# Two edits in the second block: the order of the first weight loads, and how the transposed matrix of the second inverse is made

## The reference

```python
h = rms_norm_2(x, attn_norm_w)
proj = h @ w_in                      # 2048 x 6448: RWKV part (3360 columns), GDN part (the rest)
#   RWKV: r, k, v (3 x 1024), then the low-rank inputs wd, ad, gd (288 columns); GDN: q, k, v, z, a, b
y_a = rwkv7_mixer(p_rwkv, ...)       # a recurrence over the tokens, 16 heads of 64
y_b = gdn_mixer(p_gdn, ...)          # gated delta rule in chunks of 64 tokens, 8 heads of 128:
#   sol = triangular_solve(L + eye, rhs, lower=True, unit_diagonal=True)
x = x + concatenate([y_a, y_b]) @ w_out
x = x + (silu(h2 @ w_gate) * (h2 @ w_up)) @ w_down
```

## Time and profile before

| what | value |
|---|---|
| median of three runs | 2945.02 us (2941.74 to 2945.82) |
| the profiled execution | 2943.11 us, span 2941.4 us |
| TensorE busy | 2876.3 us, 98% |
| VectorE, ScalarE busy | 54%, 40% |
| granted TensorE clock, mean | 0.99 of full speed |
| DMA | 501.12 MB, mean 170 GB/s |

### The profile page before, as it was taken

The page is one execution under the profiler, slowest core; times in us unless marked ns, Lnnn a source line. Parts: engine busy times, 40 slices in busy tenths (PEclk is TensorE's granted clock), DMA queues, the critical chain, the costliest instruction groups (busy, mean ns, idle before and its releaser), DMA issues.

```text
span 2941.4 us, 41822 instructions
## 1 busy us (share of the span) xinstructions
PE 2876.3 (98%) x18274; PEld 2480.6 (84%) x18274; DVE 1600.7 (54%) x1325; ACT 1167.7 (40%) x958; POOL 58.6 (2%) x124
## 2 busy tenths in 40 slices
PE   8999999999999999999998999988899999999998
PEld 7999888888888888888888989988788888888887
DVE  5657555444554455444447657875555445544445
ACT  4345444334443333333335343423344343333333
POOL 0000000000000000002002000000000000000000
PEclk9999999999999999999999999999899999999999
DMA  6555555656555555555565445300255555655554
GB/s 216 163 164 180 161 168 189 197 187 195 186 190 186 185 191 191 188 186 192 194 209 171 158 132 170 101 4 32 86 167 191 186 187 189 195 185 186 198 189 171
DMA packets 257411, 501.12 MB, mean 170 GB/s; under 512 B 12256, under 2 KB 17707, under 8 KB 256891
## 3 DMA queue, kind: packets, MB, share of 16 engines
q1 hardware_dynamic: 257275, 499.06, 52.3%
HBM read 496.74 MB, written 2.10 MB: 170 GB/s over the span
## 4 chain that ended last, share of the span: by engine, by line
PE 94%; DVE 4%; ACT 1%; DMA 1%; issue 0%; SPq 0%; DVEq 0%; ACTq 0%
PE psum L696 23%; PE psum L698 23%; PE psum L697 23%; PE psum L681 5%; PE psum L683 5%; PE psum L684 5%; PE psum L1130 2%; DVE weight_lo L1899 1%; PE psum L747 1%; PE psum L1011 0%; PE psum L642 0%; DMA weight_raw<-in_w_in 0%; ACT weight_hi L1427 0%; PE psum L1017 0%; PE psum L1023 0%; PE psum L996 0%
## 5 line engine op out<-in xcount | busy, mean ns | idle before, releaser
L1899 DVE TENSOR_TENSOR weight_lo<-weight_raw,weight_hi 128x2048 fp32r<-128x2048 f32 x460 | 1054.0, 2292 | 1109.3 <-ACT weight_hi L1427 1108.7
L1427 ACT ACTIVATE weight_hi<-weight_raw 128x2048 fp32r<-128x2048 f32 x460 | 881.4, 1916 | 1509.8 <-PE psum L698 1211.7
L696 PE MATMUL psum<-weight_hi,h_both 128*128 128x512 f32 x1856 | 724.9, 391 | 0.0
L698 PE MATMUL psum<-weight_hi,h_both 128*128 128x512 f32 x1856 | 722.5, 389 | 0.0
L697 PE MATMUL psum<-weight_lo,h_both 128*128 128x512 f32 x1856 | 722.1, 389 | 0.0
L681 PE MATMUL psum<-h_both,weight_hi 128*128 128x256 f32 x1408 | 403.9, 287 | 18.4 <-DVE weight_lo L1899 18.3
L698 PEld LDWEIGHTS psum<-weight_hi,h_both 128*128 128x128 f32 x1856 | 348.3, 188 | 72.8
L697 PEld LDWEIGHTS psum<-weight_lo,h_both 128*128 128x128 f32 x1856 | 348.5, 188 | 71.4
L696 PEld LDWEIGHTS psum<-weight_hi,h_both 128*128 128x128 f32 x1856 | 348.4, 188 | 71.3
L683 PE MATMUL psum<-h_both,weight_lo 128*128 128x256 f32 x1408 | 400.6, 285 | 0.0
L684 PE MATMUL psum<-h_both,weight_hi 128*128 128x256 f32 x1408 | 400.4, 284 | 0.0
(11 more groups left out here) (525 smaller groups left out, 2228.5 us busy)
## 6 DMA issues: line engine op xcount, KB each, us to landing
weight_raw<-in_w_in SPq DMA_DIRECT2D x144, 1024.0 KB, 5.3
weight_raw<-in_w_ffn_in SPq DMA_DIRECT2D x88, 1024.0 KB, 5.0
weight_raw<-in_w_ffn_out SPq DMA_DIRECT2D x44, 1024.0 KB, 5.1
weight_raw<-in_ffn_w_gate SPq DMA_DIRECT2D x44, 1024.0 KB, 5.1
weight_raw<-in_ffn_w_up SPq DMA_DIRECT2D x44, 1024.0 KB, 5.2
weight_raw<-in_ffn_w_down SPq DMA_DIRECT2D x44, 1024.0 KB, 5.1
weight_raw<-in_w_out SPq DMA_DIRECT2D x32, 1024.0 KB, 5.1
weight_raw<-in_w_branch_rnn SPq DMA_DIRECT2D x8, 1024.0 KB, 5.1
```

The lines of the kernel that those rows point to most:

```text
L696: mm(acc[:, t, :], xh[:, c], wh[:, k, :], start=(start and k == 0), stop=False, skip_group_check=True)
L698: last = mm(acc[:, t, :], xl[:, c], wh[:, k, :], start=False, stop=(stop and k == CK - 1), skip_group_check=True)
L1427: A(hi[j % g.hi][:], raw[j % g.ring][:], ACT.Copy).then_inc(hi_ready, 1)
L1899: V.tensor_tensor(lo[r][:], raw[r][:], hi[j % g.hi][:].bitcast(F32), ALU.subtract).then_inc(lo_ready, 1)
```

## The change

In SP's program the order after the fourth chunk becomes: fifth and sixth chunk; wait for `n_sq`; half of the low-rank weights (rows of the first 8 of 16 tiles of 128); seventh chunk; the other half; eighth chunk. The two DMAs become four. ACT does the high parts of chunks five to seven in one go, then waits for all of the low-rank weights (64 instead of 32) and for `x_rescaled`, and splits them in two groups of two. DVE's order there is unchanged.

In the second inverse, for k < 4, the product for the transposed matrix and its addition go, and `chunk_turn` makes the transposed matrix from the new X with a DVE transpose. Its start is made in the same way instead of by `gd_begin`; ACT's copy of `gd_nt` is no longer waited for by DVE. Step 4 stays as it was, but for its semaphores.

```diff
-            load(in2, 0, 0, 4)
+            def load_lora(p0, p1):
+                k = slice(4 * p0, 4 * p1)
+                sp.dma_start(w_lora[:, k, 0:288], w_in2[:, k, 3072:N_RWKV]).then_inc(S("lora_w_landed"), 16)
+                sp.dma_start(w_lora[:, k, 288:LC], w_in2[:, k, 6432:6448]).then_inc(S("lora_w_landed"), 16)
+
+            load(in2, 0, 0, 6)
             sp.wait_ge(n_sq, 16)
-            sp.dma_start(w_lora[:, :, 0:288], w_in2[:, :, 3072:N_RWKV]).then_inc(S("lora_w_landed"), 16)
-            sp.dma_start(w_lora[:, :, 288:LC], w_in2[:, :, 6432:6448]).then_inc(S("lora_w_landed"), 16)
-            load(in2, 0, 4)
+            load_lora(0, 2)
+            load(in2, 0, 6, 7)
+            load_lora(2, 4)
+            load(in2, 0, 7)
...
             def chunk_x(k, b):
                 pe.wait_ge(S("gd_z_out"), 2 * k + b + 1)
-                of_chunks(bank(4 + 2 * b), lambda r, u: xt_gc[r, u, :], lambda r, u: z_gc[r, u, :], 8, 8 * b)
-                of_chunks(bank(5 + 2 * b), lambda r, u: z_gc[r, u, :], lambda r, u: xt_gc[r, u, :], 8, 8 * b).then_inc(S("gd_x"), 1)
+                pe.wait_ge(S("gd_xt_out"), 2 * k + b + 1)
+                last = of_chunks(bank(4 + 2 * b), lambda r, u: xt_gc[r, u, :], lambda r, u: z_gc[r, u, :], 8, 8 * b)
+                if k == 4:
+                    last = of_chunks(bank(5 + 2 * b), lambda r, u: z_gc[r, u, :], lambda r, u: xt_gc[r, u, :], 8, 8 * b)
+                last.then_inc(S("gd_x"), 1)
...
-            chunks(in2, 0, 4, 6)
-            act.wait_ge(S("lora_w_landed"), 32)
+            chunks(in2, 0, 4, 7)
+            act.wait_ge(S("lora_w_landed"), 64)
             act.wait_ge(*at_step("x_rescaled"))
-            lora_high(0, 1)
-            chunks(in2, 0, 6, 7)
-            lora_high(1, 3)
+            lora_high(0, 2)
             chunks(in2, 0, 7, 8)
-            lora_high(3, 4)
+            lora_high(2, 4)
...
+            def chunk_turn(k, b):
+                u = slice(8 * b, 8 * b + 8)
+                dve.wait_ge(S("gd_x_out"), 2 * k + 2 + b + 1)
+                V.transpose(xt_gc[:, u, :], x_gc[:, u, :]).then_inc(S("gd_xt_out"), 1)
...
-                if g == 3:
-                    dve.wait_ge(S("gd_nt_out"), 2)
-                    gd_begin(xt_gc, nt_g, low0_t_c, 0)
+                if g >= 2:
+                    chunk_turn(-1, g - 2)
...
-            dve.wait_ge(S("gd_nt_out"), 4)
-            settle(gd_begin(xt_gc, nt_g, low0_t_c, 1))
...
             def chunk_z(k):
                 for b in range(2):
                     u = slice(8 * b, 8 * b + 8)
+                    if b and k:
+                        chunk_turn(k - 1, 1)
                     dve.wait_ge(S("gd_z"), 2 * k + b + 1)
...
                     dve.wait_ge(S("gd_x"), 2 * k + b + 1)
-                    for o, x in enumerate((x_gc, xt_gc)):
-                        last = V.tensor_tensor(x[:, u, :], x[:, u, :], bank(4 + 2 * b + o).rearrange("p (u n) -> p u n", u=8), ALU.add)
-                    last.then_inc(S("gd_x_out"), 1)
+                    for o, x in enumerate((x_gc, xt_gc) if k == 4 else (x_gc,)):
+                        V.tensor_tensor(x[:, u, :], x[:, u, :], bank(4 + 2 * b + o).rearrange("p (u n) -> p u n", u=8),
+                                        ALU.add).then_inc(S("gd_xt_out" if o else "gd_x_out"), 1)
+                if k < 4:
+                    chunk_turn(k, 0)
```

More of the change, by code:

```diff
@@ L1338, in _ @@
                 pe.wait_ge(S("gd_z_low_out"), b + 1)
+                pe.wait_ge(S("gd_xt_out"), 10 + b + 1)
                 for u in range(8):
@@ L2678, in _ @@
             chunk_x(4)
-            dve.wait_ge(S("gd_x_out"), 12)
+            dve.wait_ge(S("gd_xt_out"), 12)
             V.memset(head_rstd[UP, 0:1], 0.0).then_inc(S("gd_xt_made"), 1)
```

## The result

The changed kernel takes 2922.93 us (median of four runs, 2919.36 to 2929.0), the kernel before 2945.14 us in the same comparison: the ratio is 0.9929, with a 95% interval of 0.9908 to 0.995. That is faster by more than the 0.2% that can be told from no change. The forecast was 2924.2 us. The profiled execution took 2919.36 us, with a span of 2917.7 us; the page answers to the earlier trace rows with

A forecast was written before the change was run, and what follows sets the result against it. TensorE, busy 98% of the span, was taken as the bound. Loads 11.8 + 2.4 - 1.0 = 13.2 us plus inverse 7.6 gave 20.8 off 2943.11; with 1.9 for the median, 2924.2 us, range 2920 to 2928 (0.57).

The forecast's parts named there:

- The fifth chunk 11.8 us earlier: Start of block two: with its load ahead of the squares, TensorE starts the fifth chunk near 1584.1 instead of 1595.91.
- The fifth chunk at full clock, 2.4 us: Block two: without the stall the fifth chunk takes 5.76 us instead of 8.2, gaining 2.4 us.
- The new wait of 1.0 us: Before the sixth chunk: TensorE waits 1.0 us for its low part, which the slow fifth chunk used to cover.
- The moved DMAs cost nothing: Low-rank weights, seventh and eighth chunks, loaded behind the squares, land in time or with lateness covered: nothing subtracted.
- the 1 us to start: Transfers behind the squares: 1 us assumed before data moves, in the estimate that all of it ends at 1592.7.
- Part 2, 7.6 us: Second inverse: two of four products per step left out in steps 0 to 3, 1.9 us each, 7.6 in all.
- the same holds after step 3: Second inverse: as after step 2, the 1.9 us is gained in full and the wait keeps its length.
- The clock inside the inverse: Second inverse: possible clock changes cost up to 3.8 us or gain up to 6.4; neither taken, both waits keeping their length.

The follow-up runs named there:

- fifth only: The changed kernel with only the fifth chunk's load ahead of the squares, the sixth behind half of the low-rank weights: 2921.65 us, ratio 0.9931.
- turns alone: The kernel before with only the DVE transposes in the second inverse, loads in the old order: 2936.75 us, ratio 0.9969.
- both orders: The changed kernel with VectorE's scalar work earlier in the second inverse and its rescaling behind the sixth chunk's low part: 2910.3 us, run again 2908.57.
- loads alone: The kernel before with only the new order of the loads, the second inverse as before: 2933.83 us, ratio 0.9961.
- one piece: The changed kernel with the low-rank weights loaded whole, between the sixth and seventh chunks: 2920.08 us, ratio 0.9923.

## Why the prediction was right

It gave 2924.2 us; the two medians are 2922.93 and 2920.42, both inside the forecast's own range of 2920 to 2928. Point by point:

- **The fifth chunk 11.8 us earlier.** It starts at 1582.43 in place of 1595.91; less the 1.53 at a, 11.95 us. The forecast chain holds with each release: high part, low part, 0.14 us, matmul (each 1.6 to 1.7 us earlier than forecast, 1.53 of it from a).
- **The fifth chunk at full clock, 2.4 us.** From 1582.43 to the end, 0.80 before 1589.22, it is 5.99 us where it was 8.2: 2.2.
- **The new wait of 1.0 us.** It is 0.80 us, before the sixth chunk and behind VectorE's rescaling, as foreseen. Together 11.95 + 2.2 - 0.8 = 13.35 at the sixth chunk, and 13.16 at b, against 13.2.
- **The moved DMAs cost nothing.** So it is; no wait for a landing is in the chain. I was too careful about the narrow rows: 3.17 us in one piece, 1.98 in two, and one piece behind the sixth chunk did as well. On their size the Trainium skill's page DMA: Bandwidth & Descriptors, section "Bandwidth", asks for 1 MiB or more per transfer; the two here are 64 KB each and cost no time that TensorE shows. Two terms of this sum were loose: the bytes behind the squares are 4.6 MB (2.49 of low-rank weights, not 2.43), and the 1 us to start was assumed. No row gives it; a load without a queue takes 5.0 us to land, where 1.05 MB at 384 GB/s are 2.7. Neither is seen in the result, which had more slack than that.
- **Part 2, 7.6 us.** It is 7.60, and 7.59 alone. At the reciprocal 5.58 of it are reached (from c to it 24.49 us, where 30.07 stood before), against 5.7: steps 0 to 2 gave their 1.9 us each. That "the same holds after step 3" is wrong. From the end of the first wait to that of the second it is 12.06 us, and it was 12.03 (2046.51 to 2058.54): step 3 gained nothing. The other 2.06 us come behind the second wait. (The start of the transposed matrix by `gd_begin` was three instructions per half, not four; nothing hangs on it.)
- **The clock inside the inverse.** I took neither bound because both waits keep their length. The net is right, its way is not: step 3 ran at 1.2 GHz throughout (64 x products in 3.68 us), where before it had recovered to full clock for its x products (a granted clock of 0.96 from 2051.24 to 2056.02), and that ate the whole gain of the step. In return the 16 products behind the second wait took 2.66 us in place of 3.78, and the 32 of line 1350 2.08 in place of 2.92. In the kernel before:

```profile
2058.54 3.78 PE L1328 MATMUL psum<-gdn_b,head_rows_r 16*128 16x128 f32 x16 [2.52 <-DVE proj L2640]
```

That what the clock took and what it gave came out alike is luck: in fifth only, with the same inverse, the stretch behind the second wait is 1.5 us longer. Of this the Trainium skill's TensorE: Matmul & The Clock Gate, section "HAM oscillation — how this bites in real kernels", had the first half: where short bursts stand between waits, each starts at the low clock again. The trace agrees for the burst between the waits of 4.10 and 2.52 us; the burst in the same place before also started at 0.50, but came back to full clock within it.

What the prediction missed lies outside its steps: 2.9 us of the 23.7 by which the traces differ came without an edit, 1.53 us ahead of a and 1.38 between b and c. Between b and c eleven traces take 226.0 to 226.3 or 227.4 us, and both values come with the turns in place; one takes 229.67. The kernel before was traced with 227.41 and the changed one with 226.03. Without the 2.9 the changed span would be 2920.6 and its execution, 1.7 us longer, 2922.3, which is what the forecast's sum gave for it. The medians, too, gained more than the 20.8 us of the sum: 22.2 and 23.7 us.

## What to carry to other kernels

A load that stands behind a wait in its queue should be asked for its own release: if its buffer was free long before (here some 15 us), moving it ahead of the wait gains the whole stall, and the gain can be summed from the engines' own chain, with what the stall used to cover (here 0.80 us of rescaling) subtracted. Moving the one late load is enough; splitting what it passes brought nothing. In a chain where TensorE waits for another engine's scalar work, taking products out gained their time in the three steps ahead of the first wait and nothing in the step between the two, where the clock stayed low instead. Putting the scalar work ahead of the bulk work gained the waits and as much again in clock.

## What the runs showed of the hardware that was not expected

The granted clock fell to 0.50 while TensorE was busy without a gap: in the gate product of block two (fp32 of 128x256 and 32x256) and just behind it, for some 15 us in turns alone, and in the first run of both orders, where it cost 6.1 us between a and b (201.51 against 195.39 in the second). In loads alone it cost 1.5 us there; in the other eight traces with the new loads it stayed at 1.00 through the same instructions. The runs of one program differ by up to 10.8 us (loads alone), and their mean clock goes with it: 0.993 at 2926.88 and 2928.87, 0.990 at 2936.17 to 2937.64. With the loads of before it held once (before) and fell once (turns alone). Why it falls in one execution and not in another stays open; no edit here was aimed at it.

A DMA issue can be slow for what stands ahead of it, and not for its own size: a chunk of 1024 KB took 6.04 us to issue behind the low-rank weights in one piece (6.77 in turns alone, 6.86 in one piece) and 2.24 us behind half of them. Whether the many short rows or the bytes ahead do it is not told apart. Line 503 itself took 3.17, 2.63 in turns alone with the same order, and 2.17 us in one piece, for the same rows.
